# Scores of one head's 64 rows read where the queries lie, and the scores of two heads issued together

## What is computed

```python
# block 1: latent attention, 8 heads, 96 query/key dims, and a dilated branch of 3 groups of 8 heads, 64 dims
o_mla = mla_branch(q_mla, ckv, k_rope, positions, ...)
o_dil = dilated_branch(qkv_dil, ...)        # banded softmax attention with distance bias, per group (128,1) (512,4) (2048,16)
# block 2, layer 0: h @ w_in cut into qa, ka, va, qb, kb, vb, 8 heads of 64 dims each
oa = moba_attention(qa, ka, va)             # softmax(q.k * scale, causal) . v : with 512 tokens every block is selected
# stick-breaking, over all keys before the query:
z = einsum('bhqd,bhkd->bhqk', q, k) * scale
log_1m = where(causal, log_sigmoid(-z), 0)
log_after = cumsum(log_1m, reverse) - log_1m
w = where(causal, exp(log_sigmoid(z) + log_after), 0)
ob = einsum('bhqk,bhkd->bhqd', w, v)
```

## Time and profile before

| | us |
|---|---|
| median of 3 executions | 3068.12 |
| the profiled execution, its own time | 3062.41 |
| its span, first to last instruction | 3061.1 |
| PE busy | 2708.2 (88%) |
| DVE busy | 1222.5 (40%) |
| ACT busy | 845.7 (28%) |
| POOL busy | 511.7 (17%) |

### The profile page before, as it was taken

The page is one execution under the profiler, slowest core; times in us unless marked ns, Lnnn a source line. Parts: engine busy times, 40 slices in busy tenths (PEclk is TensorE's granted clock), DMA queues, the critical chain, the costliest instruction groups (busy, mean ns, idle before and its releaser), DMA issues. The chain is left out here.

```text
span 3061.1 us, 34956 instructions
## 1 busy us (share of the span) xinstructions
PE 2708.2 (88%) x13844; PEld 2142.3 (70%) x13844; DVE 1222.5 (40%) x2216; ACT 845.7 (28%) x1672; POOL 511.7 (17%) x595
## 2 busy tenths in 40 slices
PE   6999968689869999399899899997898899799997
PEld 5898958476555555286667687875697796587886
DVE  5533152242231111400553666525574563433333
ACT  2323231342121111110463321223422322332222
POOL 4564714300012222120000100001020110100001
PEclk9999978799979999699999899998998899899999
DMA  6332400002338999420001466522102102232322
GB/s 216 124 108 86 137 16 27 11 28 85 87 138 325 402 418 373 172 69 28 1 1 56 139 184 197 167 69 77 35 1 56 28 1 56 83 90 79 108 81 71
DMA packets 325649, 338.84 MB, mean 111 GB/s; under 512 B 19120, under 2 KB 296752, under 8 KB 313072
## 3 DMA queue, kind: packets, MB, share of 16 engines
q1 hardware_dynamic: 303280, 279.69, 27.8%
q0 software_dynamic: 22208, 56.93, 5.2%
HBM read 370.11 MB, written 16.78 MB: 126 GB/s over the span
## 5 line engine op out<-in xcount | busy, mean ns | idle before, releaser
L331 DVE TENSOR_TENSOR sb_w_lo<-sb_weights,sb_w_hi 128x1024 fp32r<-128x1024 f32 (+2 forms) x215 | 239.9, 1125 | 503.4 <-ACT sb_w_hi L325 503.2
L373 PE MATMUL bank<-sb_h_hi,sb_w_hi 128*128 128x512 f32 x1040 | 421.0, 405 | 11.6 <-DVE sb_w_lo L331 11.6
L375 PE MATMUL bank<-sb_h_hi,sb_w_lo 128*128 128x512 f32 x1040 | 408.4, 393 | 0.0
L374 PE MATMUL bank<-sb_h_lo,sb_w_hi 128*128 128x512 f32 x1040 | 407.9, 392 | 0.0
L325 ACT CAST sb_w_hi<-sb_weights 128x1024 fp32r<-128x1024 f32 x224 | 215.5, 970 | 554.4 <-PE bank L375 489.1
L414 POOL TENSOR_TENSOR sb_scratch<-sb_scratch 128x512 f32<-128x512 f32 x30 | 38.7, 1288 | 1320.5 <-ACT sb_scratch L404 1320.5
L913 PE MATMUL bank<-sb_weights,sb_hT 128*128 128x256 f32 x960 | 233.7, 400 | 14.2 <-DVE sb_padded L1361 12.3
L373 PEld LDWEIGHTS bank<-sb_h_hi,sb_w_hi 128*128 128x128 f32 x1040 | 196.8, 189 | 65.7 <-issue 25.7
L913 PEld LDWEIGHTS bank<-sb_weights,sb_hT 128*128 128x128 f32 x960 | 214.1, 286 | 23.6 <-issue 13.1
L374 PEld LDWEIGHTS bank<-sb_h_lo,sb_w_hi 128*128 128x128 f32 x1040 | 197.0, 189 | 45.6 <-issue 5.3
L375 PEld LDWEIGHTS bank<-sb_h_hi,sb_w_lo 128*128 128x128 f32 x1040 | 196.6, 189 | 43.2
(11 more groups left out here) (488 smaller groups left out, 4947.1 us busy)
## 6 DMA issues: line engine op xcount, KB each, us to landing
sb_weights<-ffn_w_in SPq DMA_DIRECT2D x88, 512.0 KB
sb_mod_weights<-ada_w POOLq DMA_DIRECT2D x24, 1024.0 KB, 5.6
sb_weights<-ada_w SPq DMA_DIRECT2D x24, 1024.0 KB
sb_expert_weights<-w_down SPq DMA_DIRECT2D x17, 1024.0 KB
sb_weights<-w_in SPq DMA_DIRECT2D x16, 1024.0 KB
sb_weights<-ffn_w_out SPq DMA_DIRECT2D x32, 512.0 KB
sb_weights<-gdn_w_in SPq DMA_DIRECT2D x32, 512.0 KB
sb_expert_weights<-w_up SPq DMA_DIRECT2D x14, 1024.0 KB
```

Source lines behind the costliest of these rows:

```text
L331: dve.tensor_tensor(u.lo[:, 0:u.kt, :], u.chunk.w, u.hi[:, 0:u.kt, :].bitcast(F32), ALU.subtract).then_inc(*k.lo.one())
L373: pe.matmul(bank[:], u.hi[:, kk, :], act[0][:, kk, :], start=first and kk == 0, stop=False)
L374: pe.matmul(bank[:], u.hi[:, kk, :], act[1][:, kk, :], start=False, stop=False)
L375: mm = pe.matmul(bank[:], u.lo[:, kk, :], act[0][:, kk, :], start=False, stop=last and kk == u.kt - 1)
```

## The change

- There is no padded tile any more. The score matmul takes 64 rows of queries and 64 rows of keys, partitions 0 to 63 for an even head and 64 to 127 for an odd one (`head_rows`). Gone are the memsets of `open_scores` with the barrier behind them, `pad_act`, `pad_dve`, and `pad_queries` with its barrier.
- In `attention_pe`, with `paired` (the three dilated groups and MoBA), step s issues the scores of jobs s and s+1 when s is even, and none when s is odd. The latent attention is called with `paired=False`.
- In the stick-breaking attention the order stays; only the operands of L2331 and L2341 have 64 rows.

```diff
+def head_rows(h):
+    return slice(h % 2 * HD, (h % 2 + 1) * HD)
...
-def attention_pe(k, jobs, padded, normalise):
+def attention_pe(k, jobs, normalise, paired=True):
     pe = k.nc.tensor
     for s in range(len(jobs) + 7):
-        if s < len(jobs):
-            j = jobs[s]
-            bank = k.bank[s % 3]
-            if s >= 3:
-                pe.wait_ge(*k.exped.at(s - 2))
-            if padded and j.h == 0:
-                pe.wait_ge(*k.padded_even.at(j.tile + 1))
-                pe.wait_ge(*k.padded_odd.at(j.tile + 1))
+        for n in (() if s >= len(jobs) else (s,) if not paired else (s, s + 1) if s % 2 == 0 else ()):
+            j = jobs[n]
+            bank = k.bank[n % 3]
+            if n >= 3:
+                pe.wait_ge(*k.exped.at(n - 2))
             mm = pe.matmul(bank[:, 0:j.n], j.query, j.keys, start=True, stop=not j.bias)
...
-                jobs.append(Job(i, h, k.padded[i % 2][:, h, :], kt[:, h // 2, lo * P:(i + 1) * P],
+                jobs.append(Job(i, h, q[head_rows(h), h // 2, i * P:(i + 1) * P],
+                                kt[head_rows(h), h // 2, lo * P:(i + 1) * P],
...
     k.arena = k.sb("arena", [P, 24 * S])
-    k.padded = [k.sb(f"padded{i}", [P, H, P]) for i in range(2)]
     k.more_weights(more)
-    for tile in k.padded:
-        k.nc.vector.memset(tile[:], 0.0).then_inc(*k.dve_step.one())
-    k.meet()
...
-                pe.matmul(k.bank[j][:, 0:S - j * P], kb[:, h // 2, j * P:(j + 1) * P], padded[:, h, j * P:S],
+                pe.matmul(k.bank[j][:, 0:S - j * P], kb[head_rows(h), h // 2, j * P:(j + 1) * P], qb[head_rows(h), h // 2, j * P:S],
...
-    jobs = [Job(i, h, k.padded[i % 2][:, h, :], ka[:, h // 2, 0:(i + 1) * P],
+    jobs = [Job(i, h, qa[head_rows(h), h // 2, i * P:(i + 1) * P], ka[head_rows(h), h // 2, 0:(i + 1) * P],
...
-    padded = k.arena[:, 4 * S:12 * S].rearrange("p (h t) -> p h t", h=H)
-    pad_queries(k, qb, padded)
-    stick_pe(k, padded, kb, vb, o)
+    stick_pe(k, qb, kb, vb, o)
```

More of the change, by code:

```diff
@@ L192, in __init__ @@
         self.sined = Count(self, "ACT", "sined")
-        self.padded_even = Count(self, "ACT", "padded_even")
         self.mixed_in = Count(self, "ACT", "mixed_in")
@@ L217, in __init__ @@
         self.mod_summed = Count(self, "DVE", "mod_summed")
-        self.padded_odd = Count(self, "DVE", "padded_odd")
         self.angled = Count(self, "DVE", "angled")
@@ L597, in attention_pe, with attention_act @@
             mm.then_inc(*k.finished.one())
-def pad_act(k, padded, i):
-    q, slots = padded
+def attention_act(k, jobs, normalise, out=None):
     act = k.nc.scalar
[L603 to L619, removed]
     for s in range(len(jobs) + 7):
-        if padded and s % 8 == 4 and s // 8 + 1 < NT:
-            pad_act(k, padded, s // 8 + 1)
         if s < len(jobs):
@@ L642, in attention_act, with attention_dve @@
                      ).then_inc(*k.mixed_in.one())
-def attention_dve(k, jobs, padded, normalise, out=None):
+def attention_dve(k, jobs, normalise, out=None):
     dve = k.nc.vector
-    if padded:
-        pad_dve(k, padded, 0)
     for s in range(len(jobs) + 7):
-        if padded and s % 8 == 4 and s // 8 + 1 < NT:
-            pad_dve(k, padded, s // 8 + 1)
         if s < len(jobs):
@@ L1001, in dilated @@
                                 (dist[:, (1 - i + lo) * P:] if g == 0 else dist, 2.0 ** -(h + 1))))
-        attention_pe(k, jobs, True, False)
-        attention_act(k, jobs, (q, k.padded), False)
-        attention_dve(k, jobs, (q, k.padded), False, outs[g])
+        attention_pe(k, jobs, False)
+        attention_act(k, jobs, False)
+        attention_dve(k, jobs, False, outs[g])
         k.meet()
@@ L1347, in mla @@
             for i in range(NT) for h in range(H)]
-    attention_pe(k, jobs, False, True)
-    attention_act(k, jobs, None, True, k.mixed[:, 0:4, :])
-    attention_dve(k, jobs, None, True)
+    attention_pe(k, jobs, True, False)
+    attention_act(k, jobs, True, k.mixed[:, 0:4, :])
+    attention_dve(k, jobs, True)
     k.meet()
@@ L2308, in groups_project, with stick_pe @@
     k.meet()
[L2314 to L2323, removed]
+def stick_pe(k, qb, kb, vb, o):
     pe = k.nc.tensor
@@ L2340, in stick_pe @@
                     pe.wait_ge(*k.act_copied.at(m - 2))
-                pe.matmul(bank[:, 0:n], kb[:, h // 2, i * P:(i + 1) * P], padded[:, h, i * P:S], start=True, stop=False)
+                pe.matmul(bank[:, 0:n], kb[head_rows(h), h // 2, i * P:(i + 1) * P],
+                          qb[head_rows(h), h // 2, i * P:S], start=True, stop=False)
                 pe.matmul(bank[:, 0:P], k.const("ident"), k.const("sb_mask"), start=False, stop=False)
@@ L2426, in head_groups @@
             for i in range(NT) for h in range(H)]
-    attention_pe(k, jobs, True, True)
-    attention_act(k, jobs, (qa, k.padded), True, k.mixed[:, 0:4, :])
-    attention_dve(k, jobs, (qa, k.padded), True)
+    attention_pe(k, jobs, True)
+    attention_act(k, jobs, True, k.mixed[:, 0:4, :])
+    attention_dve(k, jobs, True)
     k.meet()
     o = qa
-    padded = k.arena[:, 4 * S:12 * S].rearrange("p (h t) -> p h t", h=H)
-    pad_queries(k, qb, padded)
-    stick_pe(k, padded, kb, vb, o)
+    stick_pe(k, qb, kb, vb, o)
     stick_act(k)
```

## The result

The kernel before took 3067.28 us in this comparison (median of 4 runs, 3062.16 to 3071.8), the changed one 3117.11 us (median of 4, 3098.88 to 3123.45): a ratio of 1.0153, with a 95% interval of 1.0099 to 1.0208. It is slower by about 50 us where 2.8 were forecast, and outside the range of 3063 to 3080. Two more executions of it on record took 3096.85 and 3131.85 us. The profiled execution is the shortest of the four: 3098.88 us, with a span of 3097.6. Against the profiled execution of before (3062.41) that is +36.5.

The account below looks back on a forecast made before the run. PE was taken to bound MoBA and g0, DVE g1, a loop through all engines stick-breaking. Terms -4.9 - 2.8 + 10.2 + 2.2 - 2.4 + 0.5 = +2.8 on the median gave 3070.9 us, range 3063 to 3080.

Parts of the forecast that it names:

- MoBA: MoBA stage, PE-bound: four row changes a pair cost 0.66 us, sixteen pairs +10.2 us; bounds +11.9 and +6.
- g1: Dilated groups g1 and g2 together: DVE relieved of padded copies, -2.4 us in all; bounds -3.9 and +2.
- g0: Dilated group g0: two row changes a pair cost 0.28 us, a tile takes 10.15 for 9.65; +2.2 us.
- rival 1: Paired scores on different halves overlap, saving one 256-column pass a pair in g0: -2.6 us, total 3068.3; chance 0.25.
- The price of a change: Each switch between 64- and 128-row matmuls costs 0.19 us, or 0.14 after a product with values; read from the delta net.
- Memsets: Two places where memsets and their barrier hold up PE: removing them gives -2.4 and -2.5 us, sum -4.9.
- First padded copies: Start of g0, g1, g2 and MoBA: PE's first score starts 0.7 us earlier without the padded copy, -2.8 in all.
- The start of the stick-breaking attention: PE's first z score can start at 1519.02 instead of 1522.58 without padded copies and their barrier: -3.6 us.
- its 1.1 for a warm clock: Start of stick-breaking: with one idle us PE keeps full clock, so DVE's first score comes sooner, -1.1 us.
- Rival 2: Switching between halves of the rows costs as much as a size change: +8 us, total 3078.9; chance 0.18.
- Rival 3: A change is free where a single short matmul stands between longer ones: -18 us, total 3050; chance 0.08.
- Rival 4: Pairing starves DVE in g1 and g2: over +2 us instead of -2.4, total +7.2, 3075.3; chance 0.12.

## Why the prediction was wrong

**Where the sum failed: the clock.** Every term took its durations from rows at the clock of before and left the clock there. That put the cost of a lower clock at nothing, without a reason: no term and no rival asked what the change does to the clock of a stage, and the only clock in the text is that of the first z scores. The runs showed g1 at 0.52 where it had 1.00, and MoBA at 0.82 where it had 1.00. The measured growth of the stages, against the forecast:

| | forecast us | measured us | PE at half the clock, before and after, us |
|---|---|---|---|
| g0 | +2.2 | +3.3 (+18 in two other runs) | 6.8, 13.7 |
| g1 | -1.2, half of the term | +7.5 | 0, the whole stage |
| g2 | -1.2 | +6.8 | 3.4, 34.1 |
| MoBA | +10.2 | +23.3 (+36 in another run) | 0, 27.3 |
| stick-breaking, without its start | +4.1 | +6.4 | 13.6, 19.4 |

In MoBA the clock is enough for the miss: 27.3 us at half speed lose up to 13.7, and 23.3 - 13.7 = 9.6 is near the forecast. That it comes within 0.6 is in part luck, since the wait for the first exponential is in it too. In g0 the changed kernel was at half for 13.7 us and the kernel before for 5.6 of its 6.8 within the stage; the difference costs about 4 us, more than the growth of 3.3, so the forecast's +2.2 isn't left: the scores overlapped (rival 1). In g0 to g2 the growth also holds the later first exponential. For g1, PE at half the clock is the bound: a pair takes 1.99 us (from 282.86 to 284.85), so sixteen take 31.8 of its 35.1, while DVE was forecast as the bound with 1.24 a pair. The timeline of that pair in the changed kernel, which answers to the earlier trace rows:

```profile
282.86 0.80 PE L565 MATMUL bank<-sb_arena 64*128 64x128 f32 x4
283.59 0.47 PE L576 MATMUL bank<-sb_consts,sb_scratch 128*128 128x128 f32 x1
283.86 0.53 PE L586 MATMUL bank<-sb_arena,sb_scratch 128*128 128x64 f32 x2
284.18 0.42 PE L576 MATMUL bank<-sb_consts,sb_scratch 128*128 128x128 f32 x1
284.39 0.53 PE L586 MATMUL bank<-sb_arena,sb_scratch 128*128 128x64 f32 x2
```

**The price of a change** was right, as far as the full clock shows it. Before, a score with 512 keys reached its mask after 0.91 us where it followed a product with values:

```profile
1499.73 1.08 PE L564 MATMUL bank<-sb_arena,sb_padded 128*128 128x512 f32 x2
1500.64 0.38 PE L566 MATMUL bank<-sb_consts 128*128 128x128 f32 x2
```

Behind a 128-column matmul it took 0.86 (1507.18 to 1508.04). In the changed kernel it takes 1.05: 0.19 more than the 0.86, and 0.14 more than the 0.91. Three pairs there take 4.84, 5.06 and 5.95 us for 4.16, 4.38 and 5.26, and pairs with 384 keys 3.75, 3.97 and 4.85 for 3.07, 3.29 and 4.17: 0.68 more each, and 0.66 was forecast. But the prediction held the price to be the same at all 28 changes of the delta net, to 0.01. That is so for 24 of them. The other four stand at half the clock, two of them around this row (clock 0.50 from 2321.6 to 2325.6), and cost 0.29 to 0.30 each:

```profile
2322.74 2.07 PE L2832 MATMUL bank<-sb_scratch,sb_ktok 64*128 64x128 f32 x8
```

So the trace of before had a clock of 0.50 around two changes, and the question that the sum left out could have been asked there. Its bound for MoBA is a slip too: 64 changes at 0.19 are 12.2, or 11.8 without the 0.4 of tile 0, and not 11.9.

**Memsets** were right: 2.3 and 2.5 us. **First padded copies** were right for PE's start, 0.85 in g1 where 0.7 was forecast, and wrong for the stage. The prediction said that ACT's table load "follows the padded copy and moves forward with it". It fell behind the wait for the first maximum instead, and the first exponentials of the four stages come later by 2.4 us in all (0.3, 0.6, 0.7 and 0.8) where the term had PE earlier by 2.8. This is a second step that failed, up to 5 us of the miss, if the exponential sets the pace at the start (an estimate). The trace of before had the case: in the latent attention, which has no padded copy, the table load stands at 598.21 behind a wait of 2.02 us for the maximum. **The start of the stick-breaking attention** came as forecast, 3.7 us for 3.6, but its 1.1 for a warm clock did not: the clock was 1.00 until 1548.0 and then fell, with idle times of only 1.02 and 0.72 us around that point, so short waits are no warrant for the clock. A later head takes 13.41 us (from 1587.16 to 1600.57) for the 13.5 forecast, and the wait at the fourth score shrank from 1.06 to 0.63, as the changes before it were swallowed:

```profile
1595.74 0.46 PE L2306 MATMUL bank<-sb_arena 64*128 64x128 f32 x2 [0.63 <-ACT sb_scratch L2349]
```

**Rival 1**, the overlap of the halves, did happen, and larger than priced: not one pass of four but two are saved when the scores are neighbours and nobody waits. In g0 at the full clock the two scores of 256 columns take 0.63 us to the next transposition where nobody waits, for 0.49 of one score before:

```profile
158.61 0.70 PE L565 MATMUL bank<-sb_arena 64*128 64x256 f32 x4
159.24 0.44 PE L576 MATMUL bank<-sb_consts,sb_scratch 128*128 128x128 f32 x2
```

In other pairs the second score starts later and they take up to 0.94. A pair of jobs there takes 2.0 to 2.5 us, 2.25 on the mean, for the 2.5 of the forecast and the 2.3 of this rival, and 2.20 before. The Trainium skill says that tiles "operate independently" (TensorEngine Tiling (Array Packing), Key Properties), and this trace agrees, with starts 7 ns apart. The same list of the Trainium skill says that a change of mode drains the engine but not what that does to the clock. **Rival 2** falls with it: where the two scores start 7 ns apart there is no cost between one half and the other. **Rival 3** falls with the 0.68. **Rival 4** could only be tested over padded queries, where it is false. What g1 would take with 64 rows at the full clock, 6.2 to 6.5 a tile by the forecast, no run showed by itself. The run with added work comes nearest; a pair of it at the full clock, where L570 is the added matmul:

```profile
289.48 0.52 PE L565 MATMUL bank<-sb_arena 64*128 64x128 f32 x4
289.92 0.70 PE L570 MATMUL bank<-sb_consts 128*128 128x256 f32 x2
```

The two scores of 128 columns start 29 ns apart and take 0.44 us together, so they overlap as well, which the prediction had excluded. The whole pair takes 1.64 (to 291.12), so without the 0.43 of the added matmul some 1.2 would be left (an estimate) where 1.39 was forecast.

**What stays open.** Why the same code in g0 got 0.83 in one execution and 0.53 in three others, and in MoBA 27.3, 54.6 or 81.9 us at half the clock; why the unpaired MoBA lost it throughout with the same number of changes; and by which measure an empty array counts. Whether the wait for the first exponential has a part in when the clock falls in the changed kernel is open too: in g1 it falls at 268.0, within PE's idle time of 2.44 us, and no run took that wait out of the changed kernel. The runs show that frequent changes lose the clock without such a wait, that full-row work between them keeps it with one, and that one-column matmuls can lose it without a change of rows. They don't show where the border lies.

## What to carry to other kernels

Count how often the number of rows changes between matmuls, not only how many rows there are. A padded operand looks like waste, but here, in a dense stream of short matmuls, it kept the number of rows the same and g1 and MoBA at 2.4 GHz; take it away only where the matmuls are long, where two halves can stand next to each other, and where few others stand between. And read the granted clock by stage before summing durations: a sum from rows at the full clock holds only while the change leaves the clock there. Before you take an instruction out, look at what stands behind it: here a copy that cost 0.6 us had let a table load of 1.28 us run beside the first scores.

## What was not expected of the hardware

- PE with no idle time in its records (10.00 of 10.00 us busy) can be granted 0.50 for tens of microseconds. Busy matmuls are not enough where short ones of 64 and of 128 rows alternate: 56.2 us at 0.53, and 30.0 at 1.00 for the same number of instructions with 128 rows.
- Work added to a stage made it shorter: 35.1 to 32.7 us in g1.
- A change between 128 and 64 rows costs 0.19 us at the full clock and 0.29 to 0.30 at half of it.
- Where a copy stood ahead of it, the load of ACT's table ran before the first maximum was there (267.08); where none did, it came behind the wait for it, with nothing of the attention beside its 1.28 us (267.58, and 598.21 in the latent attention before). Why isn't shown.
- Two float32 matmuls of 64 rows on different halves of the array take the time of one, both passes: 1.06 us for two scores of 512 columns, and 1.05 for one.
- The clock differs between executions of the same program, in the same stage: 40.7 and 55.3 us for g0.
